# Expert weights of gate and up loaded in blocks that hold half the contraction of both, and multiplied together over 512 moving columns

## What is computed

```python
def grouped_moe(h, router_w, router_b, w_gate, w_up, w_down):
    ...
    hid = jax.nn.silu(jnp.einsum('td,edf->tef', ht, w_gate)) * jnp.einsum('td,edf->tef', ht, w_up)
    y = jnp.einsum('tef,efd->td', hid * gates[:, :, None], w_down)
```

## Time and profile before

| | before |
|---|---|
| median of 3 runs | 888.6 us (887.39 to 890.14) |
| profiled execution, first to last instruction | 884.8 us |
| median less that span | 3.8 us |
| PE busy | 812.8 us, 92% of the span |
| DVE busy | 550.0 us, 62% |
| ACT busy | 468.4 us, 53% |
| mean granted TensorE clock | 0.945 of full speed |

### The profile page before, as it was taken

One profiled execution on the slowest core, in us unless ns is written; L12 is line 12 of the kernel. 1 busy time (PEld: TensorE's weight loads), 2 busy tenths in 40 slices (PEclk: granted clock), 3 DMA queues, 4 the chain that ended last, 5 costly groups with the idle time before them and its releaser, 6 DMA issues. The chain is left out here.

```text
span 884.8 us, 14943 instructions
## 1 busy us (share of the span) xinstructions
PE 812.8 (92%) x5938; PEld 685.0 (77%) x5938; DVE 550.0 (62%) x805; ACT 468.4 (53%) x652; POOL 79.2 (9%) x103
## 2 busy tenths in 40 slices
PE   3789999989999789999999957999999799999995
PEld 2368767756787689999999934798769589999994
DVE  2253323359632887777778646674395678978885
ACT  3263221268621755656666524763484466766763
POOL 0103000710004000000000031201300200000000
PEclk9789999999999699999999975999999889999998
DMA  9896898993212057889988869973063339999942
GB/s 323 261 291 151 278 313 270 311 318 118 63 50 94 1 175 246 288 296 302 303 289 288 270 220 347 262 226 125 17 222 111 96 100 308 349 335 349 341 170 74
DMA packets 169554, 198.01 MB, mean 224 GB/s; under 512 B 15586, under 2 KB 156428, under 8 KB 169484
## 3 DMA queue, kind: packets, MB, share of 16 engines
q1 hardware_dynamic: 165120, 183.06, 65.1%
q10 hardware_dynamic: 3212, 9.81, 2.9%
q0 software_dynamic: 1152, 4.19, 1.4%
HBM read 187.61 MB, written 9.44 MB: 223 GB/s over the span
## 5 line engine op out<-in xcount | busy, mean ns | idle before, releaser
L2231 DVE TENSOR_TENSOR w_lo<-raw,w_hi 128x2048 fp32r<-128x2048 f32 x96 | 219.6, 2290 | 32.1 <-ACT w_hi L1126 31.5
L1126 ACT ACTIVATE w_hi<-raw 128x2048 fp32r<-128x2048 f32 x96 | 183.6, 1913 | 64.1 <-PE bank L1263 55.1
L1261 PE MATMUL bank<-w_hi,xg_hi 128*128 128x256 f32 x384 | 111.7, 291 | 0.6 <-DVE xg_lo L2451 0.5
L1263 PE MATMUL bank<-w_hi,xg_lo 128*128 128x256 f32 x384 | 109.3, 285 | 0.0
L1262 PE MATMUL bank<-w_lo,xg_hi 128*128 128x256 f32 x384 | 109.2, 284 | 0.0
L1261 PE MATMUL bank<-h_hi,w_hi 128*128 128x512 f32 (+2 forms) x288 | 103.5, 359 | 6.1 <-DVE h_lo L1985 4.0
L1263 PE MATMUL bank<-h_hi,w_lo 128*128 128x512 f32 (+2 forms) x288 | 101.1, 351 | 0.0
L1262 PE MATMUL bank<-h_lo,w_hi 128*128 128x512 f32 (+2 forms) x288 | 101.1, 351 | 0.0
L1928 DVE TENSOR_TENSOR w_lo<-raw,w_hi 128x2048 fp32r<-128x2048 f32 (+1 forms) x20 | 45.3, 2267 | 50.3 <-ACT w_hi L865 50.1
L865 ACT ACTIVATE w_hi<-raw 128x2048 fp32r<-128x2048 f32 (+1 forms) x20 | 37.2, 1867 | 73.7 <-PE bank L1263 56.5
L1261 PEld LDWEIGHTS bank<-w_hi,xg_hi 128*128 128x128 f32 x384 | 74.2, 193 | 0.9 <-issue 0.9
(11 more groups left out here) (323 smaller groups left out, 1590.9 us busy)
## 6 DMA issues: line engine op xcount, KB each, us to landing
raw<-in_ada_w SPq DMA_DIRECT2D x46, 1024.0 KB, 10.0
raw<-in_moe_w_gate SPq DMA_DIRECT2D x32, 1024.0 KB, 6.7
raw<-in_moe_w_up SPq DMA_DIRECT2D x32, 1024.0 KB, 6.8
raw<-in_moe_w_down SPq DMA_DIRECT2D x32, 1024.0 KB, 6.2
raw<-in_w_in SPq DMA_DIRECT2D x14, 1024.0 KB, 11.4
raw<-in_w_out SPq DMA_DIRECT2D x8, 1024.0 KB, 7.1
y_rows<-y_sb ACTq DMA_DIRECT2D x16, 512.0 KB, 4.9
ada_first<-in_ada_w SPq DMA_DIRECT2D x2, 1024.0 KB, 12.5
```

What stands on the lines that cost most here:

```text
L1126: act.activation(w_hi[slot][:, :, :], raw[q][:, :, :], ACT.Copy).then_inc(split_hi, 1)
L1261: pe.matmul(dst, w_hi_, x_hi_, start=first, stop=False)
L1263: return pe.matmul(dst, w_lo_, x_hi_, start=False, stop=last)
L2231: dve.tensor_tensor(w_lo[slot][:, :, :], raw[q][:, :, :], w_hi[slot][:, :, :].bitcast(F32), ALU.subtract).then_inc(split_lo, 1)
```

## The change

For gate and up the two blocks of an expert are cut another way. The block of role 0 now holds chunks 0 to 3 of both matrices, the block of role 1 chunks 4 to 7 of both. Each block is filled by two DMAs of 512 KB, and a second semaphore, `loaded_b[q]`, counts the second one. The contraction is dealt out as feature p*8+c on partition p and chunk c, in place of c*128+p: four chunks of one matrix are then 4 KB side by side in memory, where a piece was 1 KB. The block of down is also filled by two DMAs, its pieces are 4 KB as before.

A matmul now has gate's and up's 256 columns of one chunk as one moving operand of 512 columns (`gate_up`), and fills the whole of bank 4 (`gate_and_up`). Since chunk c must hold features p*8+c, the stationary operand of `gather` takes every eighth feature of `h_tok` (`features`: 128 floats, 32 bytes from one to the next). `wait_copies` waits for all eight chunks. The semaphores of layer 1's rounds are merged with those of layer 0 with an offset `DENSE`, which changes no wait.

```diff
+        def features(rows, c):
+            return rows.rearrange("p (f k) -> p k f", k=KC)[:, c, :]
+        def gate_up(block, c):
+            return block[:, :, :].rearrange("p (r c) n -> p r c n", r=2)[:, :, c, :]
...
-                        src = (w_gate, w_up, w_down)[role][l][bass.ds(2 * i + j, 1)]
-                        dst = raw[q][:, :, :]
-                        if role < 2:
-                            src = src.rearrange("a (k p) n -> p (a k) n", p=P)
-                        else:
-                            src = src.rearrange("a (f p) n -> p (a f) n", p=P)
-                            dst = dst.rearrange("p (f k) n -> p f (k n)", f=2)
-                        sp.dma_start(dst, src).then_inc(loaded[q], 16)
+                        for part, landed in enumerate((loaded[q], loaded_b[q])):
+                            dst = raw[q][:, 4 * part:4 * part + 4, :]
+                            if role < 2:
+                                src = (w_gate, w_up)[part][l][bass.ds(2 * i + j, 1)]
+                                src = src.rearrange("a (p k) n -> p (a k) n", k=KC)[:, 4 * role:4 * role + 4, :]
+                            else:
+                                src = w_down[l][bass.ds(2 * i + j, 1)].rearrange("a (f p) n -> p (a f) n", p=P)[:, part, :]
+                                dst = dst.rearrange("p k n -> p (k n)")
+                            sp.dma_start(dst, src).then_inc(landed, 16)
...
                     act.wait_ge(loaded[q], n * 16 + 16 * n0)
+                    act.wait_ge(loaded_b[q], n * 16 + 16 * (N_MOE // RAW) * m)
...
+            gate_and_up = bank[4][:, :].rearrange("p (r n) -> p r n", r=2)
...
                 def wait_copies(part, half, l=l):
-                    if part == 0:
-                        pe.wait_ge(q_ta, l * KC + 4 * (half + 1))
-                    else:
-                        pe.wait_ge(q_td, l * KC + (8 if half else 6))
+                    pe.wait_ge((q_ta, q_td)[part], (l + 1) * KC)
...
-                                                    h_tok[part][:, t, c * P:(c + 1) * P], onehot[:, t, :],
+                                                    features(h_tok[part][:, t, :], c), onehot[:, t, :],
...
-                                for c in range(KC):
-                                    if even and role == 0 and c % 4 == 0:
-                                        pe.wait_ge(x_hi, 2 * i + (m * E + 2))
-                                        pe.wait_ge(x_lo, 2 * i + (m * E + c // 4 + 1))
+                                if even:
+                                    pe.wait_ge(x_hi, 2 * i + (m * E + 2))
+                                    pe.wait_ge(x_lo, 2 * i + (m * E + role + 1))
+                                for c in range(4 * role, 4 * role + 4):
                                     sl = slice((j % 2) * SLOTS, (j % 2 + 1) * SLOTS)
-                                    ins = product(bank[4][:, role * FE:(role + 1) * FE], xg_hi[:, c, sl], xg_lo[:, c, sl],
-                                                  w_hi[role][:, c, :], w_lo[role][:, c, :], c == 0, c == KC - 1)
+                                    ins = product(gate_and_up, xg_hi[:, c, sl], xg_lo[:, c, sl],
+                                                  gate_up(w_hi[role], c % 4), gate_up(w_lo[role], c % 4), c == 0, c == KC - 1)
                                 ins.then_inc(used, 1)
```

More of the change, by code:

```diff
@@ L286, in build @@
         loaded = [sem(f"loaded{i}") for i in range(RAW)]
+        loaded_b = [sem(f"loaded_b{i}") for i in range(RAW)]
         s_ident = sem("s_ident")
@@ L333, in build @@
         s_ga = sem("s_ga")
-        d_p, d_gp, d_gs, d_tp, d_ta, d_tb, d_ghi, d_glo, d_xhi, d_xlo, d_s, d_m, d_t, d_th, d_tl, d_yh, d_yl, d_c, d_f, d_x = (
-            sem(n) for n in ("d_p", "d_gp", "d_gs", "d_tp", "d_ta", "d_tb", "d_ghi", "d_glo", "d_xhi", "d_xlo", "d_s", "d_m",
-                             "d_t", "d_th", "d_tl", "d_yh", "d_yl", "d_c", "d_f", "d_x"))
+        d_gp, d_gs, d_tp, d_ta, d_tb, d_yh, d_yl, d_c, d_f, d_x = (
+            sem(n) for n in ("d_gp", "d_gs", "d_tp", "d_ta", "d_tb", "d_yh", "d_yl", "d_c", "d_f", "d_x"))
         f_y, f_bias, f_eva, f_evd, f_out = (sem(n) for n in ("f_y", "f_bias", "f_eva", "f_evd", "f_out"))
@@ L350, in rounds_before @@
             return sum(ROUNDS[:l])
+        DENSE = E * rounds_before(DEPTH - 1)
         QUADS = N_ADA // 4
@@ L695, in next_layer @@
                             sp.sem_inc(loaded[q], 16 * (N_MOE // RAW) * (ROUNDS[l] - k))
+                            sp.wait_ge(loaded_b[q], 16 * (N_MOE // RAW) * m)
+                            sp.sem_inc(loaded_b[q], 16 * (N_MOE // RAW) * (ROUNDS[l] - k))
                         sp.wait_ge(split_hi, s0 - RAW + q + 1)
@@ L1205, in dense_round @@
                             for half in range(2):
-                                act.wait_ge(d_ghi, 4 * k + 2 * e + half + 1)
+                                act.wait_ge(g_hi, DENSE + 4 * k + 2 * e + half + 1)
                                 for b in range(2):
@@ L1220, in dense_round @@
                                 split_expert(l, k, 2, (e - 1) // 2, (e - 1) % 2)
-                            act.wait_ge(d_t, k * E + e)
+                            act.wait_ge(q_t, DENSE + k * E + e)
                             act.wait_ge(used, (order(2, e - 3) if e >= 3 else 0) + s0)
                             act.activation(ht_hi[(e - 1) % 2][:, :, :].rearrange("p f n -> p (f n)"), bank[5][:, 0:2 * SLOTS],
-                                           ACT.Copy).then_inc(d_th, 1)
+                                           ACT.Copy).then_inc(q_th, 1)
                         if e < E - 1:
@@ L1230, in dense_round @@
                             act.wait_ge(used, order(1, e) + s0)
-                            act.wait_ge(d_m, k * E + e)
-                            act.activation(hid_g[:, :], bank[4][:, 0:FE], ACT.Silu).then_inc(d_s, 1)
+                            act.wait_ge(q_m, DENSE + k * E + e)
+                            act.activation(hid_g[:, :], bank[4][:, 0:FE], ACT.Silu).then_inc(q_s, 1)
                         if e < E - 1:
@@ L1802, in gather @@
                             if part == 1:
-                                pe.wait_ge(d_xhi, 4 * k + 2 * i + half + 1)
+                                pe.wait_ge(x_hi, DENSE + 4 * k + 2 * i + half + 1)
                             elif i == 1:
-                                pe.wait_ge(d_xlo, 4 * k + half + 1)
+                                pe.wait_ge(x_lo, DENSE + 4 * k + half + 1)
                             for c in range(4 * half, 4 * half + 4):
@@ L1808, in gather @@
                                     ins = pe.matmul(bank[c // 2][:, (c % 2) * 2 * SLOTS:(c % 2 + 1) * 2 * SLOTS],
-                                                    h_tok[part][:, t, c * P:(c + 1) * P],
+                                                    features(h_tok[part][:, t, :], c),
                                                     onehot_g[:, t, 2 * i * SLOTS:(2 * i + 2) * SLOTS],
                                                     start=(t == 0), stop=(t == nt - 1))
-                            ins.then_inc((d_ghi, d_glo)[part], 1)
-                    pe.wait_ge(d_p, k + 1)
+                            ins.then_inc((g_hi, g_lo)[part], 1)
+                    pe.wait_ge(q_p, DENSE // 2 + k + 1)
                     if k:
@@ L1854, in dense_round @@
                                 if role == 0:
-                                    pe.wait_ge(d_m, k * E + e)
-                                for c in range(KC):
-                                    if e % 8 == 0 and role == 0 and c % 4 == 0:
-                                        pe.wait_ge(d_xhi, 4 * k + e // 4 + 2)
-                                        pe.wait_ge(d_xlo, 4 * k + e // 4 + c // 4 + 1)
+                                    pe.wait_ge(q_m, DENSE + k * E + e)
+                                if e % 8 == 0:
+                                    pe.wait_ge(x_hi, DENSE + 4 * k + e // 4 + 2)
+                                    pe.wait_ge(x_lo, DENSE + 4 * k + e // 4 + role + 1)
+                                for c in range(4 * role, 4 * role + 4):
                                     i, sl = e // 8, slice((e // 4 % 2) * SLOTS, (e // 4 % 2 + 1) * SLOTS)
-                                    ins = product(bank[4][:, role * FE:(role + 1) * FE], pair_hi[i][:, c, sl], pair_lo[i][:, c, sl],
-                                                  w_hi[role][:, c, :], w_lo[role][:, c, :], c == 0, c == KC - 1)
+                                    ins = product(gate_and_up, pair_hi[i][:, c, sl], pair_lo[i][:, c, sl],
+                                                  gate_up(w_hi[role], c % 4), gate_up(w_lo[role], c % 4), c == 0, c == KC - 1)
                                 ins.then_inc(used, 1)
@@ L1891, in dense_combine @@
                         if c == 0 and g == 0:
-                            pe.wait_ge(d_xlo, 4 * k + 4)
```

(9 more changed lines are left out.)

20 lines of the change are left out of this document (10 added, 10 removed).

## The result

The changed kernel takes 947.79 us (median of 4 runs, 945.35 to 948.99), the kernel before 888.0 us (median of 4, 886.32 to 890.14): a ratio of 1.0662, with a 95% interval from 1.0633 to 1.0692. It is slower by 59.8 us, where 885.1 us was forecast; it is rival A that happened. The profiled execution's span is 944.9 us.

The account below looks back on a forecast made before the run. PE's stream was taken to bound both layers' experts. Gate and up -3.8 plus wait +0.3 gave -3.5 us: span 884.8 to 881.3, plus 3.8 between span and median, 885.1 us; range 881 to 946.

Parts of the forecast that it names:

- rival A: Gather's strided weight load at half rate: matmul 204 to 220 ns instead of 118, 50 to 59 us more; chance 0.39.
- (2): Gather's stationary operand at 32 bytes step: weight load costs nothing extra, matmuls stay at 118 ns.
- (1): Gate and up: 768 matmuls of 512 columns at 234 ns replace pairs at 239.2 ns, saving 3.8 us.
- rival C: Gate and up's 512 columns run as quickly as the projection's, 229.5 ns: 881.7 us; chance 0.06.
- (3): Expert weight loads: 96 more DMA issues at 0.37 us on SP's queue, covered by 6.5 us, priced at nothing.
- Rival B: No measurable gain: two 256-column runs cost a pair, or DMA holds layer 1 (887.0 us); chance 0.15.
- (4): Waits: `wait_copies` asking for all eight chunks starts layer 0's first gather 0.3 us late; other waits cost nothing.

Follow-up runs that it names:

- before_strided: The kernel before with only features dealt by 8 (gather operand at 32 bytes step, all eight copies waited for), 256 columns, one DMA per block: 958.15 us, 1.076.
- step1_256: `step1_wait` with gate and up multiplied apart again, 256 moving columns each, from the same half blocks on two DMAs: 889.75 us, 0.9999.
- step1_wait: `step1` with the kernel before's waits for copies ahead of the first gather: 883.5 us, 0.9928; run again, 881.3 us, 0.9908.
- perm_write: `perm_read`, but copies read PSUM in order and write `h_tok` in SBUF at 512 bytes step: 887.24 us, 0.9982.
- before_all_copies: The kernel before with only the changed kernel's wait, all eight copies ahead of the first gather: 892.12 us, 1.0032.
- step1: The changed kernel with contiguous features (4 bytes step, 1 KB pieces), keeping 512 columns, two DMAs, new wait: 885.99 us, 0.9958; again 883.58 us, 0.9941.
- perm_read: The changed kernel with the permutation moved into copies to `h_tok`, reading PSUM at 32 bytes step; gather reads side by side: 883.82 us, 0.9933.
- step2: As `step1`, but every second feature in a chunk: gather operand at 8 bytes step, pieces of 2 KB: 886.52 us, 0.9971.
- step4: As `step1`, but every fourth feature in a chunk: gather operand at 16 bytes step, pieces of 4 KB: 945.14 us, 1.0625.

## Why the prediction was wrong

**(2), the gather's stationary operand, is the step that failed.** It priced a load at 32 bytes step at nothing, because "the path from SBUF delivers about 2.5 floats per ns", the ordinary load used half of that, and a halved path would still be enough. The transposes' 139 ns and the moving columns say what the path gives of floats side by side, and nothing of what it gives of floats in different lines. At 4 floats in a line it has room, at 2 it is just enough (199 ns), at 1 it is not: 338 ns, of which 250 are not fixed, instead of 102. The step of the loads was forecast 5 ns more at the most and measured 122 (119 for the matmuls). The page of the Trainium skill and the chance of 0.39 for A stood against it; I let an argument outweigh them that no row of the trace carried. Rival A had the mechanism, but a load at half its rate as the worst case, 220 ns a step and 944 us; 240 ns came, and 947.79 us lie past the range's 946.

**(1), gate and up, had the right mechanism and sign, but the wrong row.** I took down's 234 ns and had the projection's 229.5 ns as the best; 227.7 ns were measured: 768 x (239.2 - 227.7) = 8.8 us instead of 4.0. That is rival C's case and past its end, and it holds from the first expert to the last: wherever the clock is full, an expert's 22 steps take 227 to 229 ns each. `before_strided` less the changed kernel (10.4 us) and `step1_256` less `step1_wait` (6.2 us) lie on its two sides. Why down's stream is slower than gate and up's for the same form and columns, no run here tells.

**(3), the loads, was right:** no split waits for one, with pieces of 1 KB (`step1_wait`) or 4 KB (the changed kernel), and half blocks on two DMAs cost nothing (`step1_256`). Rival B falls.

**(4), the wait, was mis-sized.** PE stands 0.78 us ahead of the first gather instead of 0.36, 0.4 us more, where I priced 0.3. Not priced was that the clock, low at that point, then rises later; stop and rise together measured 3.2 us (1.2 to 4.5) in the kernel before. That the rise is later with the edit is shown by the profiles, five against eight; why, and why `perm_write` with the longest stop isn't the latest, stays open.

**The balance.** In the changed kernel the late clock costs nothing, since its gather goes at the same pace at either clock. PEld in two stretches of it, then of `before_all_copies` (busy us and count, clock, DMA share, GB/s):

```profile
309.10:314.10 5.00, 5.00 (x22) 0.50 0.02 5
315.10:320.10 5.00, 5.00 (x22) 1.00 0.58 210
```

```profile
306.90:311.90 5.00, 5.00 (x24) 0.50 0.02 5
313.00:318.00 5.00, 5.00 (x44) 1.00 0.60 210
```

And behind the stop for `hid_m` in layer 0 the kernel before falls to the low clock for 3.4 us, which the changed one doesn't; the two in turn (columns as in the earlier trace rows):

```profile
323.00:325.00 2.00, 2.00 (x14) 2.00 (x14) 2.00 (x2) 0.84 (x2) 0.00 (x0) 0.69 0.78 232
325.00:327.00 2.00, 2.00 (x12) 2.00 (x11) 2.00 (x4) 0.00 (x0) 0.00 (x0) 0.50 1.07 367
327.00:329.00 2.00, 2.00 (x18) 2.00 (x18) 1.30 (x1) 1.74 (x1) 0.00 (x0) 0.96 1.09 357
```

```profile
333.00:335.00 2.00, 1.37 (x7) 1.19 (x8) 2.00 (x3) 1.52 (x2) 0.00 (x0) 1.00 0.29 94
335.00:337.00 2.00, 2.00 (x11) 1.64 (x10) 2.00 (x4) 0.06 (x1) 0.00 (x0) 1.00 0.96 358
```

The sum goes by the matmuls' starts. The kernel before ran some 8 of its gather matmuls at the low clock in layer 0, where they take nearly what they take now, so 568 x 0.119 = 67.6 us come on; less 8.8 for gate and up, with 0.4 of stop, and less half of 3.4 us that are no longer at the low clock: +57.5 us. Measured are +59.8 (56.2 to 61.4 by its interval), and +58.4 in the experts' stages of the two profiles. Layer 1's clock is left aside in this, though it isn't the same: from its first gather on the kernel before stands at the low clock for 3.1 us and the changed one for 12.9, more than half of that in a gather that loses nothing by it.

For `step1_wait` the same sum says -8.8, plus the waits of its profile that grew (`hid_m` 3.4 us instead of 2.9, and `w_lo` in layer 1 0.9 instead of nothing): -7.4 us; measured are -6.0 and -7.6 us in two sets of runs. Its two profiles have the experts' stages 6.5 and 6.8 us shorter than the kernel before, but dealt out otherwise: 3.0 and 3.5 us in layers 0 and 1 of the first, with 13.1 and 3.1 us at the low clock, and 5.9 and 0.9 us in the second, with 6.0 and 9.6 (the kernel before: 8.6 and 3.1). So a few us of a stage hang on where the low clock happens to fall. The stages ahead of the experts end at another time in each profile too: one and the same kernel, `step1`, has its first gather load at 307.0 us in one and at 310.2 in the other. What the rest is stays open.

**The faster version.** `step1_wait` beats both kernels, the one before by less than 1%: contiguous features, half blocks in 1 KB pieces, 512 columns, the old waits; 0.9908 and 0.9928 in two sets. `perm_read`, with 4 KB pieces and the new wait, is at 0.9933; with the old wait it wasn't run.

## What to carry to other kernels

Before a layout change that steps through an operand of a matmul, count how many 16-byte lines its 128 elements touch: up to 64 for fp32 the load stayed under a matmul of 256 columns, from 96 on it set the pace, and a gather that is a small share of the program (576 of 5938 matmuls) cost it 7.6% (`before_strided`). If a permutation is needed, try it where a copy reads out of PSUM anyway; here it was free there. And a measured rate of contiguous access is no evidence for strided access: with a rule and an unmeasured case on one side, the argument needs a row.

## What the runs showed of the hardware

- A weight load of 128 fp32 columns at the full clock: 188, 199, 261, 331 and 338 ns at a step of 4, 8, 12, 16 and 32 bytes. In the gather, under matmuls of 256 columns, such loads start 118 to 121 ns apart at 4 bytes, and 123 ((4.02 - 0.20) / 31), 175, 233 and 240 ns apart at the others; the matmuls start 118, 120, 172, 230 and 237 ns apart.
- At 32 bytes step the gather goes at the same pace at 1.2 and at 2.4 GHz: 22 loads touch 5 us of either.
- Reading PSUM at 32 bytes step costs a copy nothing (ACT 483 ns against 482); writing SBUF at 512 bytes step makes it 818 ns.
- A stop of 0.78 instead of 0.36 us while the clock was low, ahead of a dense stream: the rise came 4.3 to 5.9 us after the stream's start (8 profiles) instead of 1.7 to 2.9 (5 profiles).

The loads' spacings at 8 and 16 bytes come from these rows, of `step2` and `step4`:

```profile
382.54 4.02 PEld L1747 LDWEIGHTS bank<-onehot,h_tok 128*128 128x128 f32 x32
```

```profile
401.20 7.54 PEld L1747 LDWEIGHTS bank<-onehot,h_tok 128*128 128x128 f32 x32
```
